# Attention in a decoder step: the causal mask moves from a bf16 matmul on TensorE to two selects on GpSimd, and GpSimd's page loads are put in step order

## The chip, the cores and the metric

One NeuronCore of a Trainium2 chip runs the whole kernel. The metric is the device time of one execution in microseconds (us); three executions of the kernel before gave 3258.64, 3258.78 and 3259.99 us, so the median is 3258.78 us.

## What is computed

One step of a one-layer hybrid decoder trunk: 2048 prompt tokens and 8 sequences of 4 sampled tokens, model width 1024. A projection gives q, k, v of 8 attention heads of width 64 and the inputs of a gated MLP; then come an output projection, a gated convolutional feed-forward part and a per-layer embedding. The change is in the attention alone. It is of the stick-breaking kind, not a softmax:

```python
def stick_breaking(q, k, v, sb_bias, q_pos, k_pos):
    z = einsum('bqhd,bkhd->bhqk', q, k) * (HEAD_DIM_SB ** -0.5) + sb_bias[None, :, None, None]
    mask = k_pos[None, :] < q_pos[:, None]
    log_1mb = where(mask, log_sigmoid(-z), 0.0)
    suffix = cumsum(log_1mb, axis=3, reverse=True) - log_1mb
    a = where(mask, exp(log_sigmoid(z) + suffix), 0.0)
    return einsum('bhqk,bkhd->bqhd', a, v)
```

In products instead of logarithms: beta = sigmoid(z), rest = sigmoid(-z), and the weight of a key is its beta times the product of rest over all later keys up to the query. A masked key has beta 0 and rest 1. The sampled tokens attend over 2048 past keys each, read from paged caches (pages of 128 keys, 256 KB each) through a page table.

## The kernel before

The program runs in stages one after the other: projections until about 577 us, the attention (`attend`) from 580 to about 1291 us, then `finish_tokens`, which is the rest. Only `attend` is changed.

**Steps.** The prompt attention is cut into 128 steps: 8 heads (h) by 16 blocks of 128 queries (i). Step s is head s // 16, block s % 16, and covers 128 * (i + 1) keys. Keys come in granules of 1024, so blocks 0 to 7 have one granule and blocks 8 to 15 have two. Every engine walks over a step counter t and works at different lags behind it:

- TensorE (PE) at t: `turn(t-3)`, which transposes the weights of step t-3 (line 998), `logits(t)` (lines 988 and 989, k in a high and a low part) and `weigh(t-4)` (line 1010), which multiplies by v. `logits` ends with the mask: a bf16 matmul (line 992) of the identity with `far_b`, whose masked entries are -2^100, is added onto the diagonal 128 columns of the logits. The next turn waits for `a_done`, the count of finished weights.
- ScalarE (ACT) at t: `sigmoid(t, g)` for each granule: beta (line 1133), then rest (line 1135), which raises `b_done`. It also copies every transposed bank out of PSUM (line 1122) and the cache sums (line 1165).
- VectorE (DVE) at t: `weights(t-2)` (line 1258, rest times beta), then `product(t-1)` (line 1253, a scan over rest from right to left). `product(s)` waits for `b_done` of the step's last granule. Now and then come `operands` (lines 1227, 1230, 1235: the next half head of q and k, which waits for a load and raises `half_ready`), sums of the sampled tokens (lines 1307 and 1310), and twice a scan and a product over 2052 columns (lines 1292 and 1296).
- GpSimd (POOL): 256 page loads in one long loop (`value_load` of the page number, then `dma_start`, line 959). Each waits until the last reader of its slot has filled its PSUM bank (`wait_filled`). Pages of keys have 8 slots, pages of values 16. Nothing on POOL takes part in the prompt's steps.

**The sampled tokens** are threaded through the same steps by `units_of[t]`: a key unit transposes two pages, a sum unit multiplies four pages of values (line 1062). By that table, written out from the code, most steps with key units free two pages, the steps with sum units free four; step 46 has three sum units (12 pages), steps 108 and 109 two each (8 pages), and steps 51 to 60 (all but 53) and 115 to 120 (all but 117) one each. Eight pages are loaded before anything else.

**The order at the start.** POOL waits for the first half of q and k (`first_loaded`), then issues loads. DVE does `product(0)` at t = 1, and behind it `operands(0, part)`, whose last part (line 1235) raises `half_ready`; on that the SyncE queue (SP) issues the load of the next q and k (line 888).

The mask matmul as it stands:

```python
if diagonal:
    d = n - P - 1024 * g
    last = nc.tensor.matmul(z[:, d:d + P], ident_b[:, :], far_b[:, :], start=False, stop=True)
last.then_inc(z_ready, 1)
```

Of the kernel before, what the change touches and what calls it, by code (L numbers as in the profile page):

```python
# [698 lines left out]


BF16 = mybir.dt.bfloat16


def attend(nc, keep, T, D, join):


# [21 lines left out]
    def granule(s, g):  # L728
        return sum(granules[:s]) + g
# [37 lines left out]
    def product_fills(t):  # L767
        fills = []
        for g, u in units_of[t] if t >= 0 else ():
            if u < KEY_UNITS and u % 4 == 3:  # L770
                fills.append(("z", g, u // 4))
            if u == U_NEW:
                fills.append(("new", g))
            if U_SUM <= u < U_MIX:
                fills.append(("sum", g, u - U_SUM))
            if u == U_MIX:
                fills.append(("mix", g))
        return fills
# [3 lines left out]
        s = t - LAG  # L782
        return min(groups[s], max(1, 3 - len(turned_fills(t)))) if has(s) else 0

    order = []
    for t in range(STEPS + LAG + 1):
        s = t - LAG
        order += turned_fills(t)
        if has(s):
            order += [("turn", s, r) for r in range(groups[s])]  # L790
        order += product_fills(t)
    fill_at = {key: n for n, key in enumerate(order)}

    with ExitStack() as ctx:
# [6 lines left out]
        aT = [m.sb(f"aT{s}", [P, 4, P]) for s in range(SLOTS)]  # L801
        bias, minus_bias = ([m.sb(f"{n}{s}", [P, 1]) for s in range(2)] for n in ("bias", "minus_bias"))
        oT = [m.sb(f"oT{s}", [64, BANK]) for s in range(2)]
        far, warm = m.sb("far", [P, P]), m.sb("warm", [P, 1])
        far_b, ident_b = m.sb("far_b", [P, P], BF16), m.sb("ident_b", [P, P], BF16)

        pages = [m.sb(f"pages{s}", [P, BANK]) for s in range(RING)]
        kT = m.sb("kT", [P, PB, 4, 2 * P])
# [14 lines left out]

        loaded, k_high, q_high, half_ready, z_ready, b_done, product_done, a_done = (
            m.sem(n) for n in ("loaded", "k_high", "q_high", "half_ready", "z_ready", "b_done", "product_done", "a_done"))
        o_ready, o_out, made, cast, rest_zeroed = (m.sem(n) for n in ("o_ready", "o_out", "made", "cast", "rest_zeroed"))
        first_loaded, first_k_high, first_q_high, first_ready, summed = (
            m.sem(n) for n in ("first_loaded", "first_k_high", "first_q_high", "first_ready", "summed"))
        filled, emptied = m.sem("filled"), [m.sem(f"emptied{b}") for b in range(3)]
# [40 lines left out]
        def slot_use(g, part, k, bi):  # L870

            n, before = page_slot(g, part, k, bi), page_loads(g, part, k, bi) - 1
            if n >= RING and k < 2 * RING // PB:
                return ("z", g, PAGES // 2 - 1)
            if before:
                last_g, last_part, last_k, last_bi = in_slot[n][before - 1]
                return ("sum", last_g, last_k) if last_part else ("key", last_g, last_k, last_bi)

        with nc.Block() as block:

# [55 lines left out]
            @block.gpsimd  # L936
            def _(pool):
                nc.gpsimd.memset(q_block[:, :, :, :], 0.0).then_inc(masks, 1)
                nc.gpsimd.memset(far[:, :], 0.0).then_inc(made, 1)
                pool.wait_ge(made, 1)  # L940
                nc.gpsimd.affine_select(out=far[:, :], in_=far[:, :], pattern=[[-1, P]], compare_op=ALU.is_gt,
                                        fill=-float(2 ** 100), base=0, channel_multiplier=1).then_inc(made, 1)
                for n in range(4):
                    nc.gpsimd.memset(rest[n][:, :].rearrange("p (k w) -> p k w", w=4 * P)[:, :, P * (n + 1) - 1:P * (n + 1)], 0.0).then_inc(rest_zeroed, 1)
                pool.wait_ge(first_loaded, 64)
                for g in range(GROUPS):
                    for part in range(2):
                        for k in range(PAGES):
                            for bi in range(PB):
                                if part == 1 and k + bi == 0:  # L950
                                    if g:
                                        wait_filled(pool, ("sum", g - 1, PAGES - 1))
                                    pool.dma_start(v_new[:, :], new_rows[16 * g:16 * g + 16, :]).then_inc(new_loaded, 16)
                                n, last_use = page_slot(g, part, k, bi), slot_use(g, part, k, bi)
                                if last_use:
                                    wait_filled(pool, last_use)
                                at = PAGES * (PB * g + bi) + k
                                page = pool.value_load(keep["page_table"][0:1, at:at + 1], min_val=0, max_val=159)
                                pool.dma_start(slots[n].unsqueeze(1), caches[part][:, bass.ds(page, 1), :]).then_inc(page_loaded[n], 16)

            @block.tensor
            def _(pe):
# [7 lines left out]
                def logits(s, g):  # L970
                    i, h = s % NQ, s // NQ
                    n = keys_of(s)
                    if s == 0:
                        pe.wait_ge(first_ready, 1)
                    if i == (4 if h == 0 else 0) and g == 0:
                        pe.wait_ge(half_ready, 2 * h + 1)
                    if i == 8 and g == 0:
                        pe.wait_ge(half_ready, 2 * h + 2)
                    at = granule(s, g)
                    z = ps_z[at % 2]  # L980
                    pe.wait_ge(b_done, at + 1)
                    width = min(n - 1024 * g, 1024)
                    for c in range(0, width, BANK):
                        w = max(min(BANK, width - c), 2 * P)
                        k0 = 1024 * g + c
                        diagonal = k0 <= n - P < k0 + w
                        q = q2[h % 2][:, i * P:(i + 1) * P]
                        nc.tensor.matmul(z[:, c:c + w], q, k_hi[h % 2][:, k0:k0 + w], start=True, stop=False)
                        last = nc.tensor.matmul(z[:, c:c + w], q, k_lo[h % 2][:, k0:k0 + w], start=False, stop=not diagonal)  # L989
                        if diagonal:  # L990
                            d = n - P - 1024 * g
                            last = nc.tensor.matmul(z[:, d:d + P], ident_b[:, :], far_b[:, :], start=False, stop=True)
                    last.then_inc(z_ready, 1)

                def turn(s, r):
# [98 lines left out]
                    if u == U_MIX:  # L1094
                        sample_mix(g)

                pe.wait_ge(cast, 2)
                for t in range(STEPS + LAG + 1):
                    s = t - LAG
                    for g, u in units_of[t]:  # L1100
# [119 lines left out]
            def _(dve):  # L1220
# [28 lines left out]

                def product(s):  # L1250
                    r = rest[s % 4][:, 0:keys_of(s) - 1][:, ::-1]
                    dve.wait_ge(b_done, granule(s, granules[s] - 1) + 3)
                    nc.vector.tensor_tensor_scan(r, r, r, 1.0, ALU.mult, ALU.min).then_inc(product_done, 1)  # L1253

                def weights(s):
# [68 lines left out]
                dve.wait_ge(masks, 1)  # L1324
                sample_masks()
                sample_queries(0)
                nc.vector.tensor_copy(ident_b[:, :], keep["ident"][:, :]).then_inc(cast, 1)
                dve.wait_ge(made, 2)
                nc.vector.tensor_copy(far_b[:, :], far[:, :]).then_inc(cast, 1)
                first_operands()  # L1330
                for t in range(STEPS + LAG + 2):
                    if has(t - 2):
# [773 lines left out]
```

## Time and profile before

| what | value |
|---|---|
| median of three executions | 3258.78 us |
| the profiled execution, its own time | 3258.63 us |
| its span, first to last instruction | 3257.0 us |
| attention within it | about 580 to 1291 us |
| TensorE busy over the span | 97% |
| VectorE, ScalarE, GpSimd busy over the span | 63%, 51%, 5% |
| mean granted TensorE clock | 0.99 of full speed |

The profile is of one execution. Busy times of TensorE overlap in part (a matmul's end is modelled), so start-to-start distances are used where a cost is read. In a timeline row the columns are start, duration (both us), engine, line, operation, out<-in, count, and in brackets the idle time before it with what ended it. A GpSimd row of line 959 shows the DMA instruction alone; the page number's read lies in the gap before it.

### The profile page before, as it was taken

How to read it: one execution, taken by the hardware profiler on the slowest of the kernel's cores; microseconds unless marked ns; L12 is line 12 of the kernel's file. 1: busy time of each engine (PE TensorE's matmuls, PEld its weight loads, DVE VectorE, ACT ScalarE, POOL GpSimd, SP SyncE). 2: the span in 40 equal slices, each digit the busy share in tenths (PEclk: the TensorE clock that was granted, in tenths of full speed). 3: DMA queues.
4: the chain of work that ended last, by engine and by line, in shares of the span. 5: the costliest groups of instructions: out<-in, count | busy, mean ns of one | idle time of the engine just before them, and what ended most of it. 6: DMA issues, size and time to landing. Idle time of an engine off the chain costs nothing.

```text
span 3257.0 us, 52028 instructions
## 1 busy us (share of the span) xinstructions
PE 3167.6 (97%) x18492; PEld 2926.9 (90%) x18492; DVE 2067.0 (63%) x2823; ACT 1654.7 (51%) x2376; POOL 149.3 (5%) x277
## 2 busy tenths in 40 slices
PE   8999899799999998999999999999999999999998
PEld 6888688688688877999999999999999999999998
DVE  4222322677887787777477764877567775678845
ACT  5434311787788877544344443544444543445433
POOL 0000000211221220000000000000000000000000
PEclk9999899899999999999999999999999999999999
DMA  5332333644554454533354333543335433443342
GB/s 171 96 99 76 105 108 102 178 116 113 168 142 123 120 141 123 168 116 113 110 163 136 116 110 113 167 132 116 115 105 180 122 116 112 134 138 116 113 120 76
DMA packets 577896, 406.03 MB, mean 125 GB/s; under 512 B 38041, under 2 KB 539202, under 8 KB 577698
## 3 DMA queue, kind: packets, MB, share of 16 engines
q1 hardware_dynamic: 536356, 300.92, 32.2%
q0 software_dynamic: 20544, 67.19, 7.2%
q10 hardware_dynamic: 20832, 35.69, 3.2%
q8 instruction: 108, 1.77, 0.2%
q14 instruction: 56, 0.46, 0.0%
HBM read 358.87 MB, written 44.87 MB: 124 GB/s over the span
## 4 chain that ended last, share of the span: by engine, by line
PE 59%; DVE 0%; DMA 0%; ACT 0%; issue 0%; ACTq 0%; DVEq 0%
PE pf_acc L60 19%; PE pf_acc L58 19%; PE pf_acc L59 19%; PE pf_ps_t L1546 1%; DMA ahead_mix<-XT 0%; PE pf_ps_sum L1485 0%; PE pf_ps_sum L1494 0%; PE pf_ps_sum L1499 0%; DVE pf_rs_sb L1864 0%; PE pf_ps_t L1556 0%; DVE pf_w_lo L1810 0%; DVE ahead_mix L1869 0%; DVE pf_h L1832 0%; DVE pf_f_lo L1880 0%; DVE pf_ssum L1826 0%
## 5 line engine op out<-in xcount | busy, mean ns | idle before, releaser
L1640 ACT ACTIVATE pf_w_hi<-ahead_raw 128x1024 fp32r<-128x1024 f32 x440 | 464.8, 1056 | 537.6 <-PE pf_acc L60 533.7
L58 PE MATMUL pf_acc<-pf_x_hi,pf_w_hi 128*128 128x416 f32 x2080 | 733.4, 353 | 2.0 <-DVE pf_h L1832 1.7
L60 PE MATMUL pf_acc<-pf_x_hi,pf_w_lo 128*128 128x416 f32 x2080 | 734.1, 353 | 0.0
L59 PE MATMUL pf_acc<-pf_x_lo,pf_w_hi 128*128 128x416 f32 x2080 | 726.0, 349 | 0.0
L1810 DVE TENSOR_TENSOR pf_w_lo<-ahead_raw,pf_w_hi 128x1024 fp32r<-128x1024 f32 x440 | 537.6, 1222 | 285.3 <-ACT pf_w_hi L1640 284.5
L58 PE MATMUL pf_acc<-pf_f_hi,pf_w_hi 128*128 128x416 f32 x1280 | 454.2, 355 | 8.9 <-DVE pf_f_lo L1877 7.2
L60 PE MATMUL pf_acc<-pf_f_hi,pf_w_lo 128*128 128x416 f32 x1280 | 452.2, 353 | 0.0
L59 PE MATMUL pf_acc<-pf_f_lo,pf_w_hi 128*128 128x416 f32 x1280 | 447.7, 350 | 0.0
L59 PEld LDWEIGHTS pf_acc<-pf_x_lo,pf_w_hi 128*128 128x128 f32 x2080 | 390.8, 188 | 7.9 <-issue 1.6
L58 PEld LDWEIGHTS pf_acc<-pf_x_hi,pf_w_hi 128*128 128x128 f32 x2080 | 390.4, 188 | 6.7 <-issue 4.6
L60 PEld LDWEIGHTS pf_acc<-pf_x_hi,pf_w_lo 128*128 128x128 f32 x2080 | 390.0, 187 | 2.3
L1253 DVE TENSOR_TENSOR_SCAN at_rest<-at_rest 128x127 f32<-128x127 f32 (+15 forms) x128 | 309.6, 2419 | 111.3 <-ACT at_rest L1135 110.7
L1010 PE MATMUL at_ps_o<-at_aT,at_v 128*64 128x128 f32 x2176 | 265.4, 276 | 6.3 <-issue 3.5
L1010 PEld LDWEIGHTS at_ps_o<-at_aT,at_v 128*64 128x64 f32 x2176 | 234.9, 137 | 22.2 <-issue 11.4
L58 PEld LDWEIGHTS pf_acc<-pf_f_hi,pf_w_hi 128*128 128x128 f32 x1280 | 240.9, 188 | 12.6 <-DVE pf_w_lo L1810 9.2
L59 PEld LDWEIGHTS pf_acc<-pf_f_lo,pf_w_hi 128*128 128x128 f32 x1280 | 241.2, 188 | 4.6 <-issue 0.8
L60 PEld LDWEIGHTS pf_acc<-pf_f_hi,pf_w_lo 128*128 128x128 f32 x1280 | 240.6, 188 | 1.6
L1122 ACT ACTIVATE at_aT<-at_ps_t 128x512 f32<-128x512 f32 (+2 forms) x320 | 160.6, 548 | 44.2 <-PE at_ps_t L998 43.8
L1133 ACT ACTIVATE at_beta<-at_ps_z,at_bias 128x1024 f32<-128x1024 f32 (+2 forms) x192 | 169.0, 880 | 16.4 <-PE at_ps_z L989 10.9
L998 PE MATMUL at_ps_t<-keep_ident,at_rest 128*128 128x128 f32 x1088 | 157.7, 279 | 18.5 <-DVE at_rest L1258 8.3
L58 PE MATMUL pa_ps_acc<-pa_w_hi,pa_x_hi 128*128 128x512 f32 x408 | 164.8, 404 | 6.8 <-DVE pa_w_lo L480 6.8
L1135 ACT ACTIVATE at_rest<-at_ps_z,at_minus_bias 128x1023 f32<-128x1023 f32 (+2 forms) x192 | 169.2, 881 | 0.0
(234 smaller groups left out, 4326.4 us busy)
## 6 DMA issues: line engine op xcount, KB each, us to landing
ahead_raw<-in_w_up_dram SPq DMA_DIRECT2D x220, 512.0 KB, 3.8
ahead_raw<-in_w_down_dram SPq DMA_DIRECT2D x80, 512.0 KB, 4.1
at_pages<-in_cache_k_dram POOLq DMA_DIRECT2D x128, 256.0 KB, 3.5
ahead_raw<-in_w_out_dram SPq DMA_DIRECT2D x40, 512.0 KB, 4.7
ahead_raw<-in_w_ple_gate_dram SPq DMA_DIRECT2D x40, 512.0 KB, 4.1
at_pages<-in_cache_v_dram POOLq DMA_DIRECT2D x64, 256.0 KB, 3.5
at_kT<-in_cache_v_dram POOLq DMA_DIRECT2D x64, 256.0 KB, 3.7
ahead_raw<-in_w_down_dram SPq DMA_DIRECT2D x40, 384.0 KB, 3.4
```

The source lines that it names most:

```text
L58: nc.tensor.matmul(out, stat_hi, mov_hi, start=first, stop=False)
L59: nc.tensor.matmul(out, stat_hi, mov_lo, start=False, stop=False)
L60: return nc.tensor.matmul(out, stat_lo, mov_hi, start=False, stop=last)
L998: last = nc.tensor.transpose(bank[:, kt % 4 * P:kt % 4 * P + P], rest[s % 4][:, kt * P:(kt + 1) * P], keep["ident"][:, :])
L1010: last = nc.tensor.matmul(ps_o[0:64, i % 4 * P:(i % 4 + 1) * P], v[h % 2][:, kt, :], aT[group(s, r) % SLOTS][:, kt % 4, :], start=kt == 0, ...
L1122: nc.scalar.activation(out, src, ACT.Copy).then_inc(emptied_by(key), 1)
L1133: nc.scalar.activation(beta[t % 3][:, 1024 * g:1024 * g + w], ps_z[at % 2][:, 0:w], ACT.Sigmoid, bias=bias[t // NQ % 2][:, :])
L1135: nc.scalar.activation(rest[t % 4][:, c0:c0 + w - skip], ps_z[at % 2][:, skip:w], ACT.Sigmoid, scale=-1.0, bias=minus_bias[t // NQ % 2][:, ...
L1253: nc.vector.tensor_tensor_scan(r, r, r, 1.0, ALU.mult, ALU.min).then_inc(product_done, 1)
L1546: done = nc.tensor.transpose(ps_t[n % NBANK_T][0:w, k * P:(k + 1) * P], h[:, 4 * half + k, tt * P:tt * P + w], keep["ident"][:, :])
L1640: nc.scalar.activation(w_hi[k % 4][:, :], raw[k % 4][:, :], ACT.Copy).then_inc(hi_split, 1)
L1810: nc.vector.tensor_tensor(w_lo[k % 4][:, :], raw[k % 4][:, :], f32(w_hi[k % 4][:, :]), ALU.subtract).then_inc(lo_split, 1)
```

## The change

The mask no longer goes into the logits. Both sigmoids are taken of the unmasked logits, and GpSimd then writes 0 into the masked part of beta's 128 diagonal columns and 1 into the masked part of rest's, each with one `affine_select` that reads and writes 128 columns in place. `product(s)` now waits for the new semaphore `masked`. `far`, `far_b`, `ident_b`, the semaphores `made` and `cast` and the two casts on VectorE go. Because POOL now serves the steps, its page loads are no longer one free-running loop: each load is put behind the mask of the step t in which its slot's last reader runs (`load_at`, never decreasing), and the first eight loads stand ahead of `mask(0)`.

```diff
-                        diagonal = k0 <= n - P < k0 + w
-                        last = nc.tensor.matmul(..., k_lo[h % 2][:, k0:k0 + w], start=False, stop=not diagonal)
-                        if diagonal:
-                            d = n - P - 1024 * g
-                            last = nc.tensor.matmul(z[:, d:d + P], ident_b[:, :], far_b[:, :], start=False, stop=True)
+                        last = nc.tensor.matmul(..., k_lo[h % 2][:, k0:k0 + w], start=False, stop=True)
...
+        load_at, latest = {}, -1
+        for page in all_pages:
+            use = slot_use(*page)
+            latest = max(latest, step_of[use] if use else -1)
+            load_at[page] = latest
...
+                def mask(s):
+                    d, i = keys_of(s) - P, s % NQ
+                    pool.wait_ge(b_done, granule(s, granules[s] - 1) + 3)
+                    b, r = beta[s % 3][:, d:d + P], rest[s % 4][:, max(d - 1, 0):d + P - 1]
+                    nc.gpsimd.affine_select(out=b, in_=b, pattern=[[-1, P]], compare_op=ALU.is_gt, fill=0.0, base=0, channel_multiplier=1)
+                    nc.gpsimd.affine_select(out=r, in_=r, pattern=[[-1, P if i else P - 1]], compare_op=ALU.is_gt, fill=1.0,
+                                            base=0 if i else -1, channel_multiplier=1).then_inc(masked, 1)
+                for page in all_pages:
+                    if load_at[page] < 0:
+                        load_page(*page)
+                for t in range(STEPS + LAG):
+                    if has(t):
+                        mask(t)
+                    for page in all_pages:
+                        if load_at[page] == t:
+                            load_page(*page)
...
-                pe.wait_ge(cast, 2)
...
-                    dve.wait_ge(b_done, granule(s, granules[s] - 1) + 3)
+                    dve.wait_ge(masked, s + 1)
                     nc.vector.tensor_tensor_scan(r, r, r, 1.0, ALU.mult, ALU.min).then_inc(product_done, 1)
...
-                nc.vector.tensor_copy(ident_b[:, :], keep["ident"][:, :]).then_inc(cast, 1)
-                dve.wait_ge(made, 2)
-                nc.vector.tensor_copy(far_b[:, :], far[:, :]).then_inc(cast, 1)
```

## Rows read from the trace of the kernel before

**Rows 1.** Windows: busy us of each engine, granted clock, DMA share and rate.

```profile
700.00:800.00 100.00, 98.39 (x854) 83.14 (x852) 76.30 (x47) 85.49 (x148) 20.72 (x37) 1.00 0.52 142
```

**Rows 2.** Waits in the attention: total us, times, longest us.

```profile
DVE at_rest L1253 <- ACT at_rest L1135: 110.7, 52, 4.4
PEld at_ps_t L998 <- DVE at_rest L1258: 20.1, 17, 4.9
```

**Rows 3.** Timeline of TensorE around the mask matmul, steps 45 and 46.

```profile
818.09 0.23 PE L992 MATMUL at_ps_z<-at_far_b,at_ident_b 128*128 128x128 bf16 x1
818.15 0.94 PE L998 MATMUL at_ps_t<-keep_ident,at_rest 128*128 128x128 f32 x7
...
824.65 0.23 PE L992 MATMUL at_ps_z<-at_far_b,at_ident_b 128*128 128x128 bf16 x1
824.81 0.43 PE L1010 MATMUL at_ps_o<-at_aT,at_v 128*64 128x128 f32 x2
```

**Rows 4.** Timeline of GpSimd: its selects, and what follows one of them.

```profile
20.14 5.78 POOL L272 TENSOR_SCALAR_AFFINE_SELECT pa_ws<-pa_ws 128x1024 f32<-128x1024 f32 x1 [11.87 <-DMA pa_bs_raw<-in_b_spatial_dram]
...
580.50 0.29 POOL L941 TENSOR_SCALAR_AFFINE_SELECT at_far<-at_far 128x128 f32<-128x128 f32 x1
580.73 0.20 POOL L944 MEMSET at_rest<- 128x4 f32 x4
```

**Rows 5.** Timeline of VectorE beside the first of these selects.

```profile
17.60 7.38 DVE L480 SCALAR_TENSOR_TENSOR pa_w_lo<-pa_w_raw,keep_cols,pa_w_hi 128x512 fp32r<-128x512 f32 x11
```

**Rows 6.** Timeline of the attention's start, several engines.

```profile
587.50 0.70 POOL L959 DMA_DIRECT2D at_pages<-in_cache_k_dram  x1 [6.56 <-issue]
...
589.65 0.42 DVE L1253 TENSOR_TENSOR_SCAN at_rest<-at_rest 128x127 f32<-128x127 f32 x1 [1.76 <-ACT at_rest L1135]
...
592.98 0.42 PE L998 MATMUL at_ps_t<-keep_ident,at_rest 128*128 128x128 f32 x1
...
595.93 0.54 POOL L959 DMA_DIRECT2D at_pages<-in_cache_k_dram  x1 [0.61 <-issue]
...
603.35 0.69 DVE L1227 CAST at_q<-at_q_raw 128x1024 fp32r<-128x1024 f32 x1 [6.41 <-DMA at_q_raw<-QT]
```

**Rows 7.** Timelines of DVE, PE and POOL, steps 40 to 47.

```profile
792.71 2.56 DVE L1253 TENSOR_TENSOR_SCAN at_rest<-at_rest 128x1151 f32<-128x1151 f32 x1 [0.57 <-ACT at_rest L1135]
...
829.67 0.54 POOL L959 DMA_DIRECT2D at_pages<-in_cache_v_dram  x1 [31.55 <-PE at_ps_t L1062]
...
835.40 1.12 PE L998 MATMUL at_ps_t<-keep_ident,at_rest 128*128 128x128 f32 x4 [4.24 <-ACT at_stage L1165]
...
845.62 4.42 DVE L1253 TENSOR_TENSOR_SCAN at_rest<-at_rest 128x2047 f32<-128x2047 f32 x1
```

**Rows 8.** Timelines of POOL, DVE and PE, steps 51 to 58.

```profile
868.75 0.54 POOL L959 DMA_DIRECT2D at_pages<-in_cache_v_dram  x1 [12.47 <-PE at_ps_t L998]
...
875.89 1.75 DVE L1253 TENSOR_TENSOR_SCAN at_rest<-at_rest 128x767 f32<-128x767 f32 x1
...
879.75 0.88 PE L998 MATMUL at_ps_t<-keep_ident,at_rest 128*128 128x128 f32 x6
...
897.64 3.08 DVE L1253 TENSOR_TENSOR_SCAN at_rest<-at_rest 128x1407 f32<-128x1407 f32 x1
...
902.12 1.61 DVE L1258 TENSOR_TENSOR at_rest<-at_rest,at_beta 128x1408 f32<-128x1408 f32 x1
...
905.92 1.42 PE L998 MATMUL at_ps_t<-keep_ident,at_rest 128*128 128x128 f32 x11
```

**Rows 9.** Timeline of PE, step 105.

```profile
1144.66 0.69 PE L998 MATMUL at_ps_t<-keep_ident,at_rest 128*128 128x128 f32 x2 [4.62 <-DVE at_rest L1258]
```

**Rows 10.** Timelines of DVE and PE, the last steps.

```profile
1214.78 1.22 DVE L1253 TENSOR_TENSOR_SCAN at_rest<-at_rest 128x511 f32<-128x511 f32 x1
...
1276.76 2.29 DVE L1258 TENSOR_TENSOR at_rest<-at_rest,at_beta 128x2048 f32<-128x2048 f32 x1
...
1281.21 2.00 PE L998 MATMUL at_ps_t<-keep_ident,at_rest 128*128 128x128 f32 x16
```

**Rows 11.** Windows behind two idle stretches of PE.

```profile
803.00:810.00 7.00, 6.99 (x42) 5.57 (x40) 6.97 (x6) 5.56 (x9) 0.00 (x0) 0.76 0.00 0
836.00:841.00 5.00, 5.00 (x18) 3.67 (x17) 4.97 (x3) 3.66 (x6) 2.14 (x4) 0.53 0.81 236
```

More of the change, by code:

```diff
@@ L698 @@
 import itertools
-BF16 = mybir.dt.bfloat16
 def attend(nc, keep, T, D, join):
@@ L783, in first_turns @@
         return min(groups[s], max(1, 3 - len(turned_fills(t)))) if has(s) else 0
-    order = []
+    order, step_of = [], {}
     for t in range(STEPS + LAG + 1):
@@ L791, in attend @@
         order += product_fills(t)
+        step_of.update({key: t for key in turned_fills(t) + product_fills(t)})
     fill_at = {key: n for n, key in enumerate(order)}
@@ L803, in attend @@
         oT = [m.sb(f"oT{s}", [64, BANK]) for s in range(2)]
-        far, warm = m.sb("far", [P, P]), m.sb("warm", [P, 1])
-        far_b, ident_b = m.sb("far_b", [P, P], BF16), m.sb("ident_b", [P, P], BF16)
+        warm = m.sb("warm", [P, 1])
         pages = [m.sb(f"pages{s}", [P, BANK]) for s in range(RING)]
@@ L825, in attend @@
             m.sem(n) for n in ("loaded", "k_high", "q_high", "half_ready", "z_ready", "b_done", "product_done", "a_done"))
-        o_ready, o_out, made, cast, rest_zeroed = (m.sem(n) for n in ("o_ready", "o_out", "made", "cast", "rest_zeroed"))
+        o_ready, o_out, masked, rest_zeroed = (m.sem(n) for n in ("o_ready", "o_out", "masked", "rest_zeroed"))
         first_loaded, first_k_high, first_q_high, first_ready, summed = (
@@ L938, in _ @@
                 nc.gpsimd.memset(q_block[:, :, :, :], 0.0).then_inc(masks, 1)
[L939 to L942, printed above, removed]
                 for n in range(4):
@@ L945, in _, with load_page @@
                 pool.wait_ge(first_loaded, 64)
[L946 to L959, printed above, removed]
+                def load_page(g, part, k, bi):
+                    if part == 1 and k + bi == 0:
+                        if g:
+                            wait_filled(pool, ("sum", g - 1, PAGES - 1))
+                        pool.dma_start(v_new[:, :], new_rows[16 * g:16 * g + 16, :]).then_inc(new_loaded, 16)
+                    n, last_use = page_slot(g, part, k, bi), slot_use(g, part, k, bi)
+                    if last_use:
+                        wait_filled(pool, last_use)
+                    at = PAGES * (PB * g + bi) + k
+                    page = pool.value_load(keep["page_table"][0:1, at:at + 1], min_val=0, max_val=159)
+                    pool.dma_start(slots[n].unsqueeze(1), caches[part][:, bass.ds(page, 1), :]).then_inc(page_loaded[n], 16)
@@ L985, in logits @@
                         k0 = 1024 * g + c
-                        diagonal = k0 <= n - P < k0 + w
                         q = q2[h % 2][:, i * P:(i + 1) * P]
                         nc.tensor.matmul(z[:, c:c + w], q, k_hi[h % 2][:, k0:k0 + w], start=True, stop=False)
-                        last = nc.tensor.matmul(z[:, c:c + w], q, k_lo[h % 2][:, k0:k0 + w], start=False, stop=not diagonal)
-                        if diagonal:
-                            d = n - P - 1024 * g
-                            last = nc.tensor.matmul(z[:, d:d + P], ident_b[:, :], far_b[:, :], start=False, stop=True)
+                        last = nc.tensor.matmul(z[:, c:c + w], q, k_lo[h % 2][:, k0:k0 + w], start=False, stop=True)
                     last.then_inc(z_ready, 1)
```

## Prediction

> **What bounds the kernel now.** I read the windows first. In a plain stretch of the attention TensorE is busy 98.39 of 100 us, VectorE 76.30 and GpSimd 20.72 [rows 1]. So TensorE sets the pace, and what is taken from it counts, as long as the others keep up. The list of waits says how well they do. VectorE's scan waits for ScalarE's sigmoid 52 times in 128 steps, 110.7 us in all: there, whatever is put between sigmoid and scan is late by its full latency. The other 76 scans find the sigmoid ready. TensorE waits for VectorE's weights only 17 times, 20.1 us [rows 2]. So the question is not how long a mask takes, but at which steps TensorE's turn has no room behind the weights. I call "room" the time from the end of `weights(s)` to the start of `turn(s)`. Going through the timeline step by step, room is 3 to 13 us in most steps. It is thin at five places: the start, steps 40 to 44, steps 52 to 58, steps 102 and 103, and steps 116 to the end.
>
> **What goes.** The mask matmul is on TensorE 128 times. A matmul's duration is mostly latency, so I take start to start: 0.06 us when a transpose follows, 0.16 us when line 1010 follows [rows 3]. There are 65 and 56 such places at full clock. Of the 0.16, 0.09 is a lead that line 1010 has behind a transpose too, so it stays. That leaves about 0.07 us a step. Upper bound: none of the lead stays; 65 x 0.06 + 56 x 0.16, and about 0.02 a step for the entry, is some 15 us (16 with the slow ones). Lower bound, nothing: where VectorE or GpSimd sets the pace. I take 0.07 us on about 85 steps where TensorE sets the pace: **-6 us**. The `far` memset and select on POOL and the two casts on VectorE ran before the first q and k had landed, so they return nothing.
>
> **What a mask costs.** A 128-column select takes 0.29 us, and the instruction behind it started 0.23 us after it [rows 4]. Two of them are 0.23 + 0.29 = 0.52, and with a hand-over of 0.03 to 0.05 us (the sigmoid ends at 589.62, the scan starts at 589.65 [rows 6]) about 0.57 us from sigmoid to scan where VectorE idles. Where VectorE is behind, the mask could run beside its work and cost nothing, or could be kept waiting by it. The only select that ran beside a busy VectorE took 5.78 us for 1024 columns [rows 4]. Eight times the columns of a 0.29 us select should be 2.3 us at most. It started at 20.14, and the unbroken chain of two-input VectorE instructions ran from 17.60 to 24.98 [rows 5]; the select ended 0.94 us after that chain. I read this as: the select got nothing until VectorE paused. Masks read SBUF in the same way, and VectorE's scans and weights have two inputs each. So in a stretch where VectorE never idles, a mask waits for it to stop, which it does only because its scan waits for the mask: about 0.5 us more on VectorE's chain for every step. The bounds are 0 (it runs beside) and 0.7 (5.78 / 8, if the long select was simply slow, twice over less overlap).
>
> The Trainium skill (page SBUF — State Buffer, section Who interferes with whom) states it as a rule: a VectorE instruction with two SBUF inputs contends with a GpSimd instruction that reads SBUF, and the second to issue waits for the whole of the first. By that rule the 0.5 us a step holds; if rows 4 were just a slow select, VectorE-bound steps would pay nothing and the sum below would be about 3263. The trace has the one instance, 5.78 us, which agrees.
>
> **What is moved.** A page load takes POOL 1.16 us from one to the next (eight first loads, 587.50 to 595.93, seven intervals of 1.2) [rows 6]. Before, only pages waited for them. Now every mask stands behind the loads of the step before, and loads stand behind masks. Two loads a step (2.3 us) fit in any step over 3 us; keys' loads are issued later by up to a step, but are needed three or more steps later, which a landing of some 4 us hides. Four, eight or twelve don't fit. Place by place:
>
> - **Start.** Eight loads end at 596.5, then `mask(0)`: the scan starts near 597.1 instead of 589.65 [rows 6]. Behind it on VectorE stand the operands, so `half_ready`, so SyncE's next load of q and k. `turn(0)` is late by 6.6 us (592.98 [rows 6]). But TensorE soon stopped anyway, until the q load had landed at 603.35 [rows 6]. That load is now asked for 7.4 us later, on queues less full. Bounds 0 (it lands no later) and 6.6 us; I take **+4**.
> - **Steps 36 to 47.** VectorE runs without idling from 792.71, and TensorE waits on its chain until 835.40 [rows 7]. Masks 36 to 40 add 2.0 us before the last idle moment is used up, masks 41 to 45 add 5 x 0.5: +4.5. Then `mask(46)`, asked for at 828, gets through only when VectorE stops at about 836.3, and its 12 loads begin at 836.7 instead of 829.67 [rows 7]. They end at 850.6, `mask(47)` at 851.2, against a scan that started at 845.62 [rows 7]: 5.6 us late, with 3.9 of room, +1.7. Together **+6.2** (bounds 0.6 and 8).
> - **Steps 51 to 58.** Four loads a step are 4.6 us, with a mask 5.2, where the steps took 3.7 to 6.6 us. From the load at 868.75, `mask(53)` ends at 878.6; its scan started at 875.89 and its turn, which had 0.1 us of room, at 879.75 [rows 8]: 2.7 us late. One step on, the mask is also held by VectorE, and POOL's lateness grows at 5.2 us a step to 6.5 us at the scan of step 58 (897.64). There the weights ended at 903.73 and the turn was at 905.92, 2.2 us of room [rows 8]: **+4.3** (bounds 2.6, without VectorE in the way, and 6.5).
> - **Steps 101 to 112.** Again an unbroken chain of VectorE (TensorE waited 4.62 us for it [rows 9]): +2.2; then eight loads at each of steps 108 and 109, whose lateness of 6.3 us meets 3.2 us of room at step 111: **+3** in all (bounds 0.6 and 5).
> - **Steps 115 to 127.** The pattern of steps 51 to 58 again, but VectorE never idles again from 1214.78 [rows 10]. Scan 121 is 6.6 us late, masks 122 to 127 add 6 x 0.5, so the last weights are 9.6 us late. They ended at 1279.05 and the last turn began at 1281.21 [rows 10]: 9.6 - 2.2 = **+7.4** (bounds 2.6 and 9).
>
> Sum: -6 + 4 + 6.2 + 4.3 + 3 + 7.4 = +18.9 us. The profiled execution took 3258.63 us, 1.6 us over its span of 3257.0 and 0.15 below the median, so I add to the median: 3258.8 + 18.9 = 3277.7, and I say **3277 us**, 0.6% slower. Nothing after the attention changes.
>
> **Rivals.** 0.2% (6.5 us) is about what a measurement of this kernel can tell from no change.
>
> 1. *Masks run freely beside VectorE* (rows 4 showed a slow form of select, not a blocked one). Only POOL's own queue is left: start 4, steps 36 to 47 0.6, 51 to 58 2.6, 101 to 112 0.6, the end 2.6, less 6: +4.4, **3263 us**, no measurable change. For it: one instance of 5.78 us is thin. Against it: that select ended just when VectorE's chain did.
> 2. *Faster.* The saving on TensorE is worth its upper bound, 16 us, and POOL gets ahead of its masks: what decides is that four loads and a mask fit into a step of about 4 us, that is, that a load costs POOL under 0.9 us and not 1.16 (its DMA instruction alone is 0.54 [rows 6]). Left are the start, 4, and 0.6 at each of four places: -16 + 6.4, **3249 us**. Against it: POOL's loads stood at 1.16 us apart wherever there was a backlog.
> 3. *Worse: new stalls drop the clock.* After TensorE idled for 2.8 and 4.2 us it was granted 0.76 of full clock over 7 us and 0.53 over 5 us, that is, 1.2 GHz for part of it [rows 11]; 1.7 and 2.4 us lost each time. Five new stalls at 2 us, and the full 6.6 at the start: +12.6 more, **3290 us**. Against it: stalls that are spread over several steps are each short.
>
> **Chances.** Forecast 0.57, rival 1 0.18, rival 2 0.10, rival 3 0.15. Faster 0.10, no change 0.18, slower 0.72. The range runs from rival 1 with twice the saving on TensorE (3255) to rival 3 with a little more (3293). The forecast's own range is 3268 to 3286.
>
> **What would show it.** No line 992; the turn directly behind line 989. Scans released by GpSimd, and where VectorE was idle, 0.57 us behind the sigmoid. Beside a busy VectorE, a select that starts or ends only at its pauses. Masks 53 and 117 behind four loads, with new idle time of TensorE ahead of line 998 near 880 and 1222 us, and the last turn some 10 to 19 us later than before. The first turn at about 599.6. I'm wrong if the selects take much longer or shorter than 0.3 us, if loads and masks overlap on POOL, or if TensorE's saving is nearer 0.16 us a step.

## The result, and the profile after

The changed kernel takes **3280.36 us** (median of four runs, 3278.52 to 3281.28), against 3258.71 for the kernel before on the same chip: ratio 1.0068 (95% interval 1.0056 to 1.0080), slower by 22 us. The profiled execution took 3280.27 us, its span is 3278.7, 21.7 more than before. The prediction said 3277 us; its sign and size held. The way to that sum held only in part, and that is what the experiments are for.

The head of the page, after:

```profile
span 3278.7 us, 52151 instructions
PE 3161.8 (96%) x18364; PEld 2923.2 (89%) x18364; DVE 2074.1 (63%) x2821; ACT 1654.6 (50%) x2376; POOL 351.5 (11%) x531
```

The windows, after, columns as in [rows 1]: a plain stretch, then the two stretches in which something broke.

```profile
700.00:800.00 100.00, 98.22 (x845) 83.45 (x843) 72.16 (x45) 86.16 (x148) 42.07 (x75) 1.00 0.50 141
800.00:900.00 100.00, 78.84 (x567) 60.70 (x565) 80.53 (x64) 63.15 (x105) 53.52 (x72) 0.90 0.43 128
1100.00:1200.00 100.00, 85.49 (x688) 71.46 (x688) 74.89 (x50) 71.03 (x118) 42.38 (x65) 0.93 0.37 103
```

In the plain stretch TensorE is as full as in [rows 1] and GpSimd has twice the work. In the two others TensorE is idle for 21 and 15 us (9 and 8 us in the same windows of the kernel before). The waits of the attention, after (us in total, times, longest), beside [rows 2]:

```profile
POOL at_beta L962 <- ACT at_rest L1145: 249.7, 84, 12.9
DVE at_rest L1263 <- POOL at_rest L963: 133.1, 91, 9.2
PEld at_ps_t L1009 <- DVE at_rest L1268: 47.4, 19, 11.8
PE at_ps_t L1009 <- DVE at_rest L1268: 37.2, 11, 11.5
```

The scan (line 1263) now waits 91 times, and for GpSimd. TensorE's waits for the weights are hardly more in number (19, 17 before), but the longest is 11.8 us, 4.9 before. Few, long stalls: that points to single steps. I took each step's `turn` (line 1009 after, 998 before) in both traces and subtracted:

| turn of step | shift, us | said |
|---|---|---|
| 0, then 8 | +6.10, +1.97 | 4 left of 6.6 |
| 39 | +0.73 | about 4 less the saving |
| **40** | **+9.35** | +6.2 spread over 36 to 47 |
| 51, 52, 53 | +9.17, +10.21, +11.81 | +4.3 by 58 |
| 62, 63 | +11.29, +11.95 | |
| 100 | +10.36 | |
| **101, 102** | **+19.33, +19.77** | +3 over 101 to 112 |
| 115, 116, 117 | +19.22, +20.29, +21.62 | |
| 124 | +21.20 | +7.4 by 127 |

The last turn starts at 1302.36 us, 1281.21 before [rows 10]: +21.15. Between the jumps the shift falls by 0.07 or 0.08 us in most steps and stays in the others; over the 82 steps behind step 8 in which it falls that is 6.0 us. It is the mask matmul's saving, as forecast. Two jumps, at steps 40 and 101, make 18 of the 21 us, and the prediction has neither. GpSimd's timeline at the first of them, after (its middle loads, 1.15 us apart, are left out):

```profile
789.65 1.24 POOL L963 TENSOR_SCALAR_AFFINE_SELECT at_rest<-at_rest 128x128 f32<-128x128 f32 x1
790.83 1.21 POOL L955 DMA_DIRECT2D at_pages<-in_cache_v_dram  x2
792.66 0.54 POOL L955 DMA_DIRECT2D at_kT<-in_cache_v_dram  x1 [0.62 <-issue]
...
800.75 0.54 POOL L955 DMA_DIRECT2D at_kT<-in_cache_v_dram  x1 [0.62 <-issue]
801.30 0.31 POOL L962 TENSOR_SCALAR_AFFINE_SELECT at_beta<-at_beta 128x128 f32<-128x128 f32 x1
801.54 0.30 POOL L963 TENSOR_SCALAR_AFFINE_SELECT at_rest<-at_rest 128x128 f32<-128x128 f32 x1
```

VectorE and TensorE in the same stretch, after:

```profile
801.88 2.65 DVE L1263 TENSOR_TENSOR_SCAN at_rest<-at_rest 128x1151 f32<-128x1151 f32 x1 [7.41 <-POOL at_rest L963]
...
810.32 1.33 DVE L1268 TENSOR_TENSOR at_rest<-at_rest,at_beta 128x1152 f32<-128x1152 f32 x1
...
811.71 2.18 PE L1009 MATMUL at_ps_t<-keep_ident,at_rest 128*128 128x128 f32 x9 [11.51 <-DVE at_rest L1268]
814.12 0.63 PE L1003 MATMUL at_ps_z<-at_k_lo,at_q 128*128 128x512 f32 x1
```

Read it upward. The turn of step 40 waits 11.51 us for the weights, these for the scan, the scan for the select at 801.54, and the select for ten page loads that stand between `mask(39)` and `mask(40)`: two of `at_pages` and eight of `at_kT`. ScalarE had finished the sigmoid at 793.49. The scan of this step started at 792.71 before [rows 7]. Step 101 is the same picture behind the ten loads of step 100: sigmoid done at 1142.56, select at 1150.98. Why ten: in steps 39 and 100 the last key unit of a group goes through. It frees two key slots, and the eight spare value slots in `kT` come free with it. I had counted the steps of twelve, eight and four loads, and not these two. Having stopped for 11.51 us, TensorE then ran at half clock for a while: it was granted 0.50 over 810 to 815 us, and the 512-column matmul at 814.12 took 0.63 us, 0.40 at full clock. Each shift compares one profiled execution of either kernel.

### The profile page after: what moved, and what is told of

It is laid out like the page before. It is cut to its first block, busy times and chain, and to the rows that moved or that the text cites. A ratio compares the mean times of both kernels' runs of the same rounds, so it can differ in the third digit from the quotient of the medians.

```text
span 3278.7 us, 52151 instructions
## 1 busy us (share of the span) xinstructions
PE 3161.8 (96%) x18364; PEld 2923.2 (89%) x18364; DVE 2074.1 (63%) x2821; ACT 1654.6 (50%) x2376; POOL 351.5 (11%) x531
## 4 chain that ended last, share of the span: by engine, by line
PE 59%; DVE 0%; DMA 0%; ACT 0%; issue 0%; ACTq 0%; DVEq 0%
PE pf_acc L60 19%; PE pf_acc L58 19%; PE pf_acc L59 19%; PE pf_ps_t L1553 1%; DMA ahead_mix<-XT 0%; PE pf_ps_sum L1492 0%; PE pf_ps_sum L1501 0%; PE pf_ps_sum L1506 0%; DVE pf_rs_sb L1871 0%; PE pf_ps_t L1563 0%; DVE pf_w_lo L1817 0%; DVE ahead_mix L1876 0%; DVE pf_f_lo L1887 0%; DVE pf_ssum L1833 0%; DVE pf_h L1839 0%
## 5 line engine op out<-in xcount | busy, mean ns | idle before, releaser
L1009 PEld LDWEIGHTS at_ps_t<-keep_ident,at_rest 128*128 128x128 f32 x1088 | 123.9, 143 | 85.8 <-DVE at_rest L1268 47.4
```

Source lines behind the costliest of these rows:

```text
L1009: last = nc.tensor.transpose(bank[:, kt % 4 * P:kt % 4 * P + P], rest[s % 4][:, kt * P:(kt + 1) * P], keep["ident"][:, :])
```

## The experiments

Before the first run there were three theories. **Q**, queue: masks stand behind page loads on GpSimd, and where many loads fall into one step the whole chain is late. **P**, port: a select and a VectorE instruction hold each other up, so every step costs VectorE time. **L**, late pages: the loads themselves are later than before, and TensorE waits for them. All ratios are against the kernel before on the same chip.

**1. Only the ten-load steps (`e1_burst`).** The loads of steps 39 and 100 go out two a step:

```diff
+        for full in (39, 100):
+            for n, page in enumerate([page for page in all_pages if load_at[page] == full]):
+                load_at[page] = full + n // 2
```

> Only the ten page loads behind mask(39) and the ten behind mask(100) are spread, two a step. Theory Q (masks stand in GpSimd's queue behind bursts of page loads): the two jumps of TensorE's turns, 8.7 us at step 40 and 9.0 us at step 101, shrink to 1 to 2 us each; about 3265 us (3262 to 3268). Theory P (a select is held up by VectorE's use of SBUF, and VectorE by the select): nothing of that is touched, 3280 us. Theory L (pages issued late land late): the last loads are issued later still, 3280 us or more.

Measured: 3264.67 us, ratio 1.0020 (1.0011 to 1.0030). Turn 40 is +2.59 against the kernel before, turn 39 being +0.98, and the second jump is 1.26 (turn 100 +3.50, turn 102 +4.76). So 16 us of the 22 were these two steps, as theory Q had it.

**2. Only the start (`e2_start`).** Of the first eight loads two go ahead of each of the masks 0 to 3:

```diff
+        for n, page in enumerate(all_pages[:8]):
+            load_at[page] = n // 2 - 1
```

> The first eight page loads are put two each ahead of mask(0), mask(1), mask(2) and mask(3). Theory Q: the first turn is back near 593 us and the 2 us that were left of the delay by step 8 go; about 3278 us (3276 to 3279). Theory P: no change, 3280 us. Theory L: the pages of steps 6 and 7 land later, up to 2 us slower.

Measured: 3276.21 us, ratio 1.0052 (1.0035 to 1.0069). That is 5 us better than the change by the ratios, 3.2 us by the medians, each against its own kernel before, and the two intervals overlap. More came back than had been lost: turn 0 is at -0.80, turn 3 at -1.87 and turn 4 at -3.35 against the kernel before. Of each, 0.9 us lie ahead of the attention (its first cast of q began at 584.99 us, at 585.93 before), which no edit here touches. Another 0.9 us, up to turn 3, is the q load for which TensorE stops [rows 6]: from its issue to the cast that waits for it are 9.0 us here, 10.4 in the kernel before, where page loads go out beside it without a pause. The last 1.5 us, from turn 3 to turn 4, is TensorE's clock: in the kernel before it had waited 2.61 us ahead of turn 3 and was then granted 0.64 of full clock up to turn 4 (4.75 us); here it had waited 0.47 us and was granted 1.00 (3.26 us).

**3. All loads spread, twice (`e3_spread`, `e5_spread2`).** Both keep the order of the loads and cap how many go behind one mask, by the length of the step; the first eight as in `e2_start`:

```diff
+        room = {0: 4, 1: 4, 2: 4, 3: 4, 4: 1, 5: 1, 6: 2, 7: 2, 8: 3, 9: 4, ..., 14: 4, 15: 5}    # e3_spread
+        room = {0: 4, 1: 4, 2: 4, 3: 4, 4: 2, 5: 2, 6: 3, 7: 3, 8: 4, 9: 4, ..., 14: 4, 15: 5}    # e5_spread2
...
+        for t in range(-1, STEPS + LAG):
+            waiting += [page for page in all_pages if freed[page] == t]
+            for page in waiting[:room[t % NQ] if t >= 0 else 2]:
+                load_at[page] = t
+            waiting = waiting[room[t % NQ] if t >= 0 else 2:]
```

> The page loads after each mask are capped by the length of the step (1 in short steps, 4 or 5 in long ones, and 2 for the first eight); what doesn't fit goes to the next step. Theory Q: all five delays go but for about 1 us each in the stretches where VectorE never idles, and the 9 us of the mask matmul come out; 3255 us (3251 to 3260). Theory P: 3276 to 3280 us. Theory L: new waits of TensorE for pages near steps 57 to 61, 3262 us or more.

Measured: 3265.97 us, ratio 1.0026 (1.0016 to 1.0035), not better than `e1_burst`. Up to turn 58 the kernel is 3.4 us ahead of the kernel before; then turn 59 is +4.57 and turn 60 +7.06. TensorE's and GpSimd's timelines of `e3_spread` there:

```profile
914.98 1.94 PE L1085 MATMUL at_ps_t<-at_kT,at_rest_s 128*32 128x512 f32 x8 [6.10 <-DMA at_kT<-in_cache_v_dram]
```

```profile
902.48 2.82 POOL L974 TENSOR_SCALAR_AFFINE_SELECT at_beta<-at_beta 128x128 f32<-128x128 f32 x1
905.26 1.27 POOL L975 TENSOR_SCALAR_AFFINE_SELECT at_rest<-at_rest 128x128 f32<-128x128 f32 x1
906.48 1.61 POOL L967 DMA_DIRECT2D at_kT<-in_cache_v_dram  x3
```

Here theory L does hold, and I made it: with caps this tight, three pages of values are left over for one step ahead of their use, and a select held up for 2.82 us delays them further. `e5_spread2` has looser caps.

> As e3_spread, with looser caps (2 and 3 loads in steps of blocks 4 to 7, 4 from block 8 on), so that no page is issued less than two steps ahead of its use; in e3_spread three were issued one step ahead and TensorE's turns went from 3.4 us early to 7 us late between steps 58 and 60. Theory L for that stretch: the 10 us come back and the time is 3256 us (3253 to 3259). If the 10 us had another cause, 3265 us again.

Measured: 3257.36 us, ratio 0.9997 (0.9988 to 1.0006). Turn 4 is at -2.54, turn 39 -3.40, turn 124 -0.63. The late pages are gone, and so is the whole loss of 22 us: with the loads laid out around the masks the kernel is level with the one before. That doesn't make the masks free. Without the matmul and with nothing in its place (`e6_nomask`, below) the time is 6.4 us under the kernel before, and this order of loads without selects (`e9_order2`) is 2.5 us under it. If the two add up, which no run tests, the selects still cost some 8 us here, and 4 of these come back in `e8_writes2`.

**4. Masks that only write (`e4_writes`, `e8_writes2`).** Both selects become memsets of the same 128 columns, so the diagonal block is left out of the attention:

```diff
-                    nc.gpsimd.affine_select(out=b, in_=b, ...)
-                    nc.gpsimd.affine_select(out=r, in_=r, ...).then_inc(masked, 1)
+                    nc.gpsimd.memset(b, 0.0)
+                    nc.gpsimd.memset(r, 1.0).then_inc(masked, 1)
```

> The two selects become two memsets of the same columns (zeros into all of beta's diagonal columns, ones into rest's), which write and do not read; the diagonal block is left out of the attention. The queue is as in the changed kernel. Theory Q: the two big jumps stay; 3277 to 3280 us. Theory P: the lengthened selects (0.8 to 4 us beside a busy VectorE) are all back at 0.2 us and most of the loss goes; 3262 us or less.

Measured, in the changed kernel: 3276.77 us, ratio 1.0055 (1.0038 to 1.0072). The two jumps stay, 8.3 us at step 40 and 8.8 at step 101, so they need no select that reads. Under the change it is 4 us by the ratios, 2.7 by the medians and 1.6 by the last turn, with overlapping intervals. In `e5_spread2`:

> e5_spread2 with the two selects replaced by memsets, which write and do not read (the diagonal block is left out of the attention). What is left of the selects' cost once the queue is short: theory P in the size that the changed kernel's trace shows, 0.1 to 0.2 us a step where VectorE never idles, gives 2 to 4 us less than e5_spread2; with my 0.5 us a step it would be 8 us or more; with no effect of reads, 0 to 1 us.

Measured: 3253.14 us, ratio 0.9983 (0.9973 to 0.9992), 4.2 us under `e5_spread2` on the same chip; the slowest of its ten runs is faster than the fastest of the other's eleven. The groups of GpSimd by form, of the kernel after and of `e4_writes` (count, then busy us in all, mean ns of one, idle before):

```profile
L962 POOL TENSOR_SCALAR_AFFINE_SELECT at_beta<-at_beta 128x128 f32<-128x128 f32 x128 | 100.1, 782 | 250.0 <-ACT at_rest L1145 249.7
L963 POOL TENSOR_SCALAR_AFFINE_SELECT at_rest<-at_rest 128x128 f32<-128x128 f32 x120 | 91.0, 758 | 0.0
L963 POOL TENSOR_SCALAR_AFFINE_SELECT at_rest<-at_rest 128x127 f32<-128x127 f32 x8 | 19.4, 2421 | 0.0
```

```profile
L962 POOL MEMSET at_beta<- 128x128 f32 x128 | 26.9, 210 | 337.4 <-ACT at_rest L1144 337.3
L963 POOL MEMSET at_rest<- 128x128 f32 x120 | 24.9, 208 | 0.0
L963 POOL MEMSET at_rest<- 128x127 f32 x8 | 1.8, 220 | 0.0
```

A select that reads takes 0.29 us when VectorE is idle, and by group 0.76 to 2.4 us in the mean; the memsets of `e4_writes` took 0.20 to 0.23 us, whatever VectorE did. VectorE's side shows in the scans of steps 118 to 127, where it never idles. Against the kernel before they fall behind by a further 1.44 to 1.47 us in four kernels with selects in all steps (the changed kernel, `e1_burst`, `e5_spread2`, `e11_both`), 0.16 us a step, and not at all with memsets (-0.01 us in `e4_writes`, -0.02 in `e8_writes2`). So P is real, but small. How much of the 4.2 us is this and how much the shorter instruction (0.21 us against 0.29) no run separates. The place is seen in the timelines of the kernel after, `mask(16)` beside the scan and the weights of step 15: GpSimd, then VectorE.

```profile
669.74 2.11 POOL L962 TENSOR_SCALAR_AFFINE_SELECT at_beta<-at_beta 128x128 f32<-128x128 f32 x1
671.81 2.44 POOL L963 TENSOR_SCALAR_AFFINE_SELECT at_rest<-at_rest 128x127 f32<-128x127 f32 x1
```

```profile
667.34 4.42 DVE L1263 TENSOR_TENSOR_SCAN at_rest<-at_rest 128x2047 f32<-128x2047 f32 x1 [2.52 <-POOL at_rest L963]
671.80 2.29 DVE L1268 TENSOR_TENSOR at_rest<-at_rest,at_beta 128x2048 f32<-128x2048 f32 x1
674.28 0.42 DVE L1263 TENSOR_TENSOR_SCAN at_rest<-at_rest 128x127 f32<-128x127 f32 x1 [0.19 <-POOL at_rest L963]
```

The first select ends (671.85) when the scan does (671.76), the second (674.25) just behind the weights (674.09). It is so throughout: all 69 selects of the kernel after that began during a scan or a product, more than 0.31 us before its end, ended 0.08 to 0.16 us after it. VectorE's durations are those of before (4.42 us for 2047 columns, 2.29 for 2048 [rows 7, 10]). The Trainium skill (page SBUF — State Buffer, section Who interferes with whom) says that a VectorE instruction with two SBUF inputs contends with a GpSimd instruction that reads SBUF and not with one that only writes it; the trace agrees with both halves (0.76 to 2.4 us against 0.21).

**5. The order alone (`e7_order`, `e9_order2`).** The kernel before, mask matmul and all, with GpSimd's loads put behind the same points in the steps as after (`e7_order`) or as in `e5_spread2` (`e9_order2`), but no selects. Of `mask(s)` only the wait is there:

```diff
+                def mask(s):
...
+                    pool.wait_ge(b_done, granule(s, granules[s] - 1) + 3)
...
+                for t in range(STEPS + LAG):
+                    if has(t):
+                        mask(t)
+                    for page in all_pages:
+                        if load_at[page] == t:
+                            load_page(*page)
```

> The kernel before, mask matmul and all, with the changed kernel's page loads: each behind a wait for the sigmoids of the step in which its slot is freed. No mask stands in GpSimd's queue. Theory Q: moving the loads costs nothing by itself, 3258 us (3256 to 3260). Theory L: later loads make TensorE wait for pages, 3264 us or more.

Measured: 3258.41 us, ratio 0.9998 (0.9988 to 1.0007). From step 3 on the shift of the turns stays between +0.3 and +0.6. So L falls for the change as made: the moved loads cost nothing by themselves, ten in one step included. In the kernel after itself TensorE's longest wait for a page was 1.1 us, 1.5 in the kernel before. The bursts cost only because a mask stands behind them.

> The kernel before with the mask matmul and with e5_spread2's order of page loads, no selects. In e5_spread2 the turn of step 3 was 1 us earlier than before and that of step 4 2.5 us, because fewer page loads stood in front of the next q load. If that is the load order's doing, this kernel has it too: 3255 us (3253 to 3257). If it was the selects' or the missing matmul's, 3258 us.

Measured: 3255.42 us, ratio 0.9994 (0.9985 to 1.0003), inside the range expected if the load order did it, but no change that can be told. The turns are at -2.2 at step 4, -1.6 from step 8 to 44, -2.7 from step 46 to 102 and -1.8 at the end, 0.9 of it again ahead of the attention. The spread start is worth 1 us at most where no mask stands behind it.

**6. The matmul alone (`e6_nomask`, `e11_both`).** The kernel before without its mask and with nothing in its place, and the kernel after with the mask matmul put back in addition:

```diff
-                        if diagonal:
-                            d = n - P - 1024 * g
-                            last = nc.tensor.matmul(z[:, d:d + P], ident_b[:, :], far_b[:, :], start=False, stop=True)
```

> The kernel before without the mask matmul and with nothing in its place: the diagonal block stays unmasked. The worth of the matmul by itself. Predicted 0.07 us on the steps where TensorE sets the pace: 6 to 8 us faster than before, 3250 to 3252 us. If the whole 0.16 us in front of line 1010 came back: 3243 us. If TensorE's saving were lost in later waits: 3258 us.

Measured: 3251.34 us, ratio 0.9978 (0.9969 to 0.9988), so -7.2 us from the ratio, -6.4 from the medians of that chip. Turn 124 is at -7.4, of which 1.4 us lie ahead of the attention.

> The changed kernel with the mask matmul put back beside the selects. What the matmul's absence was worth inside the changed kernel: with 0.07 us a step where TensorE sets the pace, 5 to 7 us slower than the changed kernel, 3284 to 3287 us. If waits had taken the saving back: 3280 us.

Measured: 3283.93 us, ratio 1.0084 (1.0069 to 1.0100), so 5 us over the change by the ratios, 4.3 by the medians, each against its own kernel before; the intervals of the two overlap, and the profiled turns say 3.25 at step 124. Between its jumps the turns of this kernel no longer gain on the kernel before. Both ways the matmul is worth 3 to 7 us.

The turns show where the two pairs differ. Without the matmul 1.2 us are gained over steps 8 to 35 in both pairs, and 2.2 and 2.3 over steps 63 to 124. Over steps 35 to 63 it is a gain of 1.9 in the kernel before and a loss of 0.5 in the changed one, and most of this gap falls on one turn, 45, behind a stop of TensorE of more than 4 us: there `e6_nomask` gains 1.1 us on the kernel before, and `e11_both` 0.7 us on the changed kernel. What differs is how long half clock lasted. In the kernel before, all eight 512-column matmuls behind the stop took 0.63 us or more; in `e6_nomask` the last three took 0.39. That is no effect of the matmul, as `e9_order2`, which keeps it, gains 1.1 us at the same turn.

**7. Masks by place (`e10_hybrid`).** Selects where TensorE sets the pace (steps 3 to 35 and 64 to 99, 69 in all), the matmul in the other 59, loads as in `e5_spread2`:

```diff
+    def by_select(s):
+        return 3 <= s < 36 or 64 <= s < 100
```

> A select only where VectorE idles and no burst of loads stands in front of it (steps 3 to 35 and 64 to 99, 69 of 128), the mask matmul in the other 59, page loads as in e5_spread2. Both theories: 69 x 0.075 = 5.2 us saved on TensorE, 2 us at the start, nothing lost to the queue or to held-up selects: 3251 us (3249 to 3254), faster than either kernel. If the selects cost something in plain steps too: 3255 us or more.

Measured: 3253.31 us, ratio 0.9989 (0.9980 to 0.9998). It is the fastest complete kernel here: turn 39 is at -4.33 and turn 99 at -6.8 against the kernel before, 0.8 of both ahead of the attention. The gain is 0.11% and its interval ends just short of 1; it is 2.1 us under `e9_order2` on the same chip, inside the expected range.

## Why the prediction came out as it did

**The sum held by two errors of opposite sign, that is, by luck.** For the two stretches with a jump the prediction had 9.2 us, and 18 were measured; for the start and the two stretches with four loads a step it had 15.7, and 7.7 were measured. Shifts of the turns, us:

| term | said | measured | |
|---|---|---|---|
| mask matmul gone | -6 | 0.07 or 0.08 in 82 steps, -6.0; -6.4 alone (`e6_nomask`) | right |
| start | +4 | +2.0 (+2.5 without the 0.5 ahead of the attention) | too much, within its bounds |
| steps 36 to 47 | +6.2 | +8.6 at step 40, then nothing | wrong in kind |
| steps 51 to 63 | +4.3 | +2.6 at 52 and 53, +0.7 at 63 | lower bound right, growth miscounted |
| steps 101 to 112 | +3 | +9.4 at 101 and 102 | wrong in kind |
| steps 115 to 127 | +7.4 | +2.4 at 116 and 117 | lower bound right, growth miscounted |

**What bounds the kernel** was read rightly: TensorE's room behind the weights decides. The jumps at 40, 52, 53, 116 and 117 fell at places that the prediction called thin. The one at 101 fell one step ahead of its list (turn 101 had 0.36 us of room), and turn 63, with 1.96 us, wasn't on it. It also named the class of cause, that every mask stands behind the loads of the step before.

**The step that failed first is the count of the loads.** The prediction's "Four, eight or twelve don't fit. Place by place" went over steps 46, 51 to 58, 108, 109 and 115 on; steps 39 and 100, with ten each, were not among the steps listed from the table of units. With the prediction's own price they come out nearly right: mask 39 ended at 790.89, ten loads at 1.16 us are 11.6 us, so mask 40 would end at 803.0. The scan of step 40 had started at 792.71, and turn 40 had no room (its wait for the weights was among the ones of [rows 2]). The trace has the scan at 801.88, since the second of the ten followed the first, behind a held select, after 0.67 us. It was no unknown of the hardware, but a step not counted. `e1_burst` shows it: without these two bursts 16 of the 22 us are gone.

**The step that failed second is the 0.5 us a step on VectorE's chain.** It was charged to masks 41 to 45, to the chain from step 101 and to masks 122 to 127, 7.7 us in all, besides the 2.0 us of masks 36 to 40. The behaviour was as described: beside a busy VectorE a select ends only with VectorE's instruction. The price was not. Over steps 121 to 127 the scans' shift grows from 22.04 to 23.14, 0.18 us a step, which the 2.2 us of room at the last turns [rows 10] just take up (0.15 us are left at turn 127); from turn 41 to turn 51 nothing is added (+9.52, then +9.17). I had taken it that a select gets in only when VectorE stops for it, and costs VectorE its whole 0.5 us. The rows of step 15 show that each select ends with the VectorE instruction beside it: the first leaves VectorE standing for 0.04 us between scan and weights, 0.03 in the kernel before, and the second costs it the 0.19 us ahead of the next scan. What all of this costs over the whole kernel is 4.2 us by `e8_writes2` and 1.6 to 4 by `e4_writes`, the shorter instruction included, not 7.7.

**Mask 46 and its twelve loads** were to cost 1.7 us. Mask 46 began at 837.52, right behind its sigmoid and in spite of a busy VectorE, and ended at 842.09. The loads were over at 852.64, 10.6 us later and not 13.9. Scan 47 is 9.47 us late, as much as the steps around it. The term is zero.

**The start** took 2.0 us, not 4. The next q load was issued at 599.99 us instead of 592.99, 7.0 later as said, but its cast began at 606.39 instead of 603.35 [rows 6], 3.0 later: issue to cast went from 10.4 to 6.4 us. GpSimd issued no page load between 595.38 and 603.04 us there; the prediction had this as "on queues less full" and let it take off only 2.6 of the 6.6 us. Turn 3 is accordingly 3.0 us late. What brought it down to 1.55 at turn 4 is the clock, which the prediction didn't have here: the stretch from turn 3 to turn 4 in the windows of the kernel before and of the kernel after,

```profile
604.93:609.68 4.75, 4.75 (x24) 3.90 (x25) 4.71 (x4) 4.75 (x8) 0.00 (x0) 0.64 1.00 303
607.97:611.23 3.26, 3.26 (x22) 2.52 (x23) 3.16 (x3) 3.26 (x6) 2.14 (x3) 1.00 0.63 224
```

took 4.75 us at 0.64 of full clock, behind a wait of 2.61 us, and 3.26 us at full clock, behind a wait of 0.76.

**Steps 51 to 58 and 115 to 120.** Four loads and a mask in a step shorter than 5.2 us did make TensorE wait at turns 52, 53, 116 and 117, with 2.6 and 2.4 us, about the lower bound. The lateness did not grow from there, for a reason that lies in the prediction's own table: steps 53 and 117 have no loads. "POOL's lateness grows at 5.2 us a step" counts four there too. By the same prices without them, POOL needs 0.6 + 4 x 5.2 = 21.4 us from mask 53 to mask 58, where the scans before took 21.75, and 0.6 + 3 x 5.2 = 16.2 from mask 117 to mask 121 against 16.44: some 2.4 us late at both, not 6.5 and 6.6. In the trace mask 54 (887.56) follows directly on mask 53. Loads behind a held select went out faster besides (below). What did grow is VectorE's lateness at 0.2 us a step: the scans' shift goes from 11.76 us at step 53 to 13.78 at step 63, the room takes it up until turn 63, and there 0.7 us come through.

**The rivals.** Rival 1 would have given 3263; with the two bursts added (about 17 us) it comes to 3280. As a total it was wrong, and its mechanism too: masks don't run freely beside VectorE, they only cost it little. Rival 2 is out: where there was a backlog loads stood 1.14 us or more apart, save behind a held select (below). Rival 3, the clock, was seen (0.84 of full clock over 804 to 844 us, 0.94 in the matching 40 us before), but in those stretches VectorE sets the pace: turn 40 is at +9.35 and turn 51 at +9.17, so it cost no time that can be seen. At the start it is the kernel before that pays for it, as shown above.

**Three smaller slips.** The wait of TensorE at 835.40 [rows 7] was ended by ScalarE's copy of a cache sum, not by VectorE's chain. Rival 1 with twice the saving is 3257 us, not 3255. And one sign of being wrong did come: the selects took 0.82 us in the mean, not 0.3.

**What stays open:** whether the selects can be placed so that they never meet VectorE, which would be worth up to 4 us; what the rest of the 8 us is that they cost in `e5_spread2`; and what remains, beside the clock at turn 45, of the difference between the matmul's worth in the changed kernel (`e11_both`) and in the one before (`e6_nomask`). The matmul's time may be hidden where a mask sets the pace, but no run separates it.

## What to carry to other kernels

When work that others wait for is put onto a queue that so far ran free, list for every step what else that queue issues, by program and not by pattern, and look at the largest entries first: two of 128 steps made 16 of these 22 us, and three added lines took them away. A helper engine's instruction that is held up by a chain can cost that chain far less than its own length (here 0.16 us a step for two selects) and the helper's queue far more (up to 4.4 us for one). Keep such a queue's work evenly spread, but not to the point at which a transfer is issued a step ahead of its use.

## What the runs showed of the hardware

- A select that reads SBUF (0.29 us alone) lasted up to 4.4 us beside VectorE's scans and products; a memset of the same columns stayed at 0.21 us (`e4_writes`). VectorE's own scans and products kept their durations, to 0.15 us each.
- Behind a held select GpSimd's loads come out faster than their 1.15 us: five in 2.68 us after mask 46 of the kernel after, where the later ones are 1.15 us apart or more. It looks as if the reads of the page numbers had gone on while the select was held, but no row shows them.

```profile
838.22 3.87 POOL L963 TENSOR_SCALAR_AFFINE_SELECT at_rest<-at_rest 128x128 f32<-128x128 f32 x1
842.04 2.68 POOL L955 DMA_DIRECT2D at_pages<-in_cache_v_dram  x5
844.87 0.54 POOL L955 DMA_DIRECT2D at_pages<-in_cache_v_dram  x1 [0.15 <-issue]
846.03 0.54 POOL L955 DMA_DIRECT2D at_pages<-in_cache_v_dram  x1 [0.62 <-issue]
```

- Behind a stop TensorE was granted about half clock for a while, and how long differed from run to run: 0.69 of full clock over the 8.6 us from 835.40 in the kernel before, 0.50 over 810 to 815 us in the kernel after.
- The q load took 10.4 us from issue to cast among page loads, and 6.4 us behind them. Issued 7.0 us later, it was cast 3.0 us later.
